# Twelve slots for split weights instead of thirteen, six raw weight buffers instead of four

## What is computed

```
h = RMSNorm(x);  proj = h @ w_in
o_gla  = gated linear attention(proj), chunks of 64, 4 heads, state carried over 16 chunks
o_diff = differential attention(proj), 4 heads, two softmax maps per head
x = x + concat(norm(o_gla) * silu(gate), norm(o_diff) * silu(gate)) @ w_out
k, v = RMSNorm(mem) @ w_ckv
x = x + softmax(RMSNorm(x) @ w_cq @ k^T) @ v @ w_co
out = RMSNorm(x)
```

## Time and profile before

| | |
|---|---|
| median of 3 runs | 870.24 us (870.15 to 870.57) |
| the profiled execution: its own time | 874.1 us |
| its span, first to last instruction | 872.4 us |
| TensorE matmul busy | 850.4 us, 97% |
| DVE busy | 529.6 us, 61% |
| ACT busy | 397.2 us, 46% |
| DMA queue of the data | 66.85 MB, 24.2% of 16 engines |
| granted TensorE clock, mean | 0.996 |

### The profile page before, as it was taken

The page is one execution under the profiler, slowest core; times in us unless marked ns, Lnnn a source line. Parts: engine busy times, 40 slices in busy tenths (PEclk is TensorE's granted clock), DMA queues, the critical chain, the costliest instruction groups (busy, mean ns, idle before and its releaser), DMA issues.

```text
span 872.4 us, 12997 instructions
## 1 busy us (share of the span) xinstructions
PE 850.4 (97%) x4676; PEld 705.0 (81%) x4676; DVE 529.6 (61%) x1274; ACT 397.2 (46%) x982; POOL 44.1 (5%) x84
## 2 busy tenths in 40 slices
PE   7999999999999999999999899999999999999997
PEld 6777877777788888888878887888888888888885
DVE  6667667767578668678768765223336654355543
ACT  7765444444346345445545655203425543234422
POOL 2000000000000000000000000000100000010001
PEclk9999999999999999999999999999999999999999
DMA  8321112112212112102112266521022202351112
GB/s 270 110 78 37 31 41 69 37 43 67 59 31 55 35 34 56 34 22 67 43 63 74 88 213 216 184 86 61 32 89 74 68 29 73 97 192 49 49 49 97
DMA packets 53592, 67.69 MB, mean 78 GB/s; under 512 B 5844, under 2 KB 32536, under 8 KB 53528
## 3 DMA queue, kind: packets, MB, share of 16 engines
q1 hardware_dynamic: 53528, 66.85, 24.2%
HBM read 58.44 MB, written 8.39 MB: 77 GB/s over the span
## 4 chain that ended last, share of the span: by engine, by line
PE 78%; DVE 11%; ACT 4%; issue 3%; DMA 3%; POOL 0%; SPq 0%; POOLq 0%; ACTq 0%
PE bank L1350 12%; PE bank L1352 12%; PE bank L1351 12%; PE banks2to L1350 8%; PE banks2to L1352 8%; PE banks2to L1351 8%; PE banks6to L1401 4%; PE banks2to L1573 4%; PE bank L1599 2%; DVE w_lo L1004 2%; DVE state L1183 1%; ACT junk L789 1%; ACT w_hi L793 1%; DMA tile_a<-mixed 1%; DVE mix_out L1207 1%
## 5 line engine op out<-in xcount | busy, mean ns | idle before, releaser
L1350 PE MATMUL bank<-w_hi,actT_hi 128*128 128x512 f32 x472 | 189.8, 402 | 1.2 <-DVE gate L1161 0.3
L1352 PE MATMUL bank<-w_hi,actT_lo 128*128 128x512 f32 x472 | 184.5, 391 | 0.0
L1351 PE MATMUL bank<-w_lo,actT_hi 128*128 128x512 f32 x472 | 184.3, 390 | 0.0
L1004 DVE SCALAR_TENSOR_TENSOR w_lo<-w_raw,vecs,w_hi 128x512 fp32r<-128x512 f32 x120 | 86.6, 747 | 43.5 <-ACT w_hi L793 43.5
L1350 PEld LDWEIGHTS bank<-w_hi,actT_hi 128*128 128x128 f32 x472 | 88.9, 188 | 22.2 <-DVE gate L1161 3.5
L1352 PEld LDWEIGHTS bank<-w_hi,actT_lo 128*128 128x128 f32 x472 | 88.6, 188 | 19.2
L1351 PEld LDWEIGHTS bank<-w_lo,actT_hi 128*128 128x128 f32 x472 | 88.9, 188 | 16.6
L793 ACT ACTIVATE w_hi<-w_raw,vecs 128x512 fp32r<-128x512 f32 x120 | 82.4, 717 | 11.8 <-DMA w_raw<-in_w_cq 6.1
L1350 PE MATMUL banks2to<-w_hi,actT_hi 128*128 128x512 f32 x168 | 66.5, 396 | 0.0
L1352 PE MATMUL banks2to<-w_hi,actT_lo 128*128 128x512 f32 x168 | 65.6, 390 | 0.0
L1351 PE MATMUL banks2to<-w_lo,actT_hi 128*128 128x512 f32 x168 | 65.5, 390 | 0.0
(11 more groups left out here) (288 smaller groups left out, 1818.9 us busy)
## 6 DMA issues: line engine op xcount, KB each, us to landing
w_raw<-in_w_in SPq DMA_DIRECT2D x56, 256.0 KB, 2.9
w_raw<-in_w_ckv SPq DMA_DIRECT2D x32, 256.0 KB, 3.4
w_raw<-in_w_cq SPq DMA_DIRECT2D x32, 256.0 KB, 2.8
w_raw<-in_w_co SPq DMA_DIRECT2D x32, 256.0 KB, 2.7
stage_in<-in_x SPq DMA_DIRECT2D x8, 512.0 KB, 4.9
tile_a<-mixed SPq DMA_DIRECT2D x16, 256.0 KB, 3.6
w_raw<-in_w_out SPq DMA_DIRECT2D x16, 256.0 KB, 3.1
x_res<-in_x SPq DMA_DIRECT2D x8, 512.0 KB, 4.9
```

Of the source, the lines that this page charges most:

```text
L1004: return dve.scalar_tensor_tensor(dst, src, scale, hi.bitcast(F32), ALU.mult, ALU.subtract)
L1350: pe.matmul(dst, l_hi, r_hi, start=start, stop=False)
L1351: pe.matmul(dst, l_hi, r_lo, start=False, stop=False)
L1352: return pe.matmul(dst, l_lo, r_hi, start=False, stop=stop)
```

## The change

Two constants change. A slot is w_hi and w_lo of a tile, 2 x 2 KB in each partition, and a raw buffer is 2 KB, so the memory that is given up and taken is the same.

```
-NW = 13
-NRAW = 4
+NW = 12
+NRAW = 6
```

## The result

The changed kernel takes 876.04 us (median of 4 runs, 875.55 to 876.53) against 870.19 us of the kernel before on the same chip (4 runs, 869.77 to 870.57): ratio 1.0065, 95% interval 1.005 to 1.0079. It is slower by 5.85 us, where 2.1 was forecast, and beyond the upper end of the range. The profiled execution of it took 875.55 us, its span is 873.8 us and its mean granted clock 0.999.

A forecast was written before the change was run, and what follows sets the result against it. The prediction took TensorE as the bound nearly everywhere. Costs of +4.15 us (+1.33 - 0.50 + 2.0 + 0.66 + 0.66) and gains of -2.05 (-1.2 - 0.85) gave +2.1 on 870.24: 872.3 us, range 869.6 to 874.7.

The forecast's parts named there:

- +1.33 - 0.50 = 0.83: GLA passes: a fourth w_lo at either end costs 1.33 us; one step per pass without a w tile returns 0.50.
- the price of a place: Bunches on TensorE's path at GLA ends, head turns, groups 6 to 7 and 14 to 15: 0.66 us per added w_lo.
- All other bunches of four: Bunches at X, C, the other Q, and V: w_lo keeps up with TensorE, so they cost 0.
- the -1.2 and the half of -1.7 against it: tile_a wait near 529 us: earlier load gives -1.2 us; avoided half clock gives -1.7, counted half as -0.85.
- rival A: Wait and clock dip near 529 us are not in timed runs, or tile lands as late: 874.4 us; chance 0.23.
- The step on the load's start: Last tile_a load starts 1.1 to 1.2 us earlier; gain bounds 0, if the tile lands as late, and -2.0.
- a wait that the prediction counted as 0: Earlier tile_a waits at 509.55 and 513 us: gain counted as 0, ends 0 and -1.1.
- The signs that the prediction named: Third tile_a wait 0.5 to 1.0 us, clock 1.00 through 531 to 535; a remaining dip would point to A.
- the clock "stayed": Clock did not fall behind waits of 1.2 us at 492.28 and 0.85 at 509.55, so 0.8 should keep it.
- Rival B: Everything in the last transfer's shadow returns, with the clock: +0.45, 870.7 us, no change; chance 0.24 together with D.
- rival C: Stage 478 to 545 us: 5.4 us idle and 1.7 dip could go, against 4.15: -2.9, 867.3 us; chance 0.08.
- Rival D: The three turns of a head absorb their tile: sum +0.1, 870.3 us; chance 0.24 together with B.

The follow-up runs named there:

- second profile of the kernel before: The kernel before, unchanged, traced a second time: 870.87 us against 870.63, ratio 1.0003, span 869.1 us.
- places alone: The kernel before with thirteen slots and four raw buffers kept, tiles placed as for twelve slots: 878.62 us, ratio 1.009 to the kernel before.
- the tile put back: The changed kernel with the second early tile of groups 4, 5 and 6 behind E 1 instead of E 2: 876.16 us, ratio 1.006 to the kernel before.
- the second set: Experiments on the cost terms one by one; its yardstick, the changed kernel unchanged, took 877.65 us, ratio 1.0074 to the kernel before.
- the load ahead of the tiles: The kernel before with tiles 80 to 82 placed behind the load of tile_a in SP's queue: 870.07 us, ratio 0.9995.
- slots alone: The kernel before with twelve slots instead of thirteen, raw buffers left at four: 877.37 us, ratio 1.0082.
- the fifth tile ahead of the last projection: The changed kernel with the fifth tile of groups 2 and 3 ahead of a GLA pass's last projection: 877.7 us, ratio 1.0077 to the kernel before.
- three places eased: The changed kernel with E 1 restored, a group 7 tile behind PV 28, tile_a's load ahead of tiles 80 to 82: 876.25 us, ratio 1.0058 to the kernel before.

## Why the prediction was wrong

The places at which the same matmul stands in the second profile of the kernel before and in the profile after give the cost stretch by stretch. Rows of the second profile of the kernel before:

```profile
212.94 0.35 PE L1524 MATMUL banks6to<-v,sc_hi 128*128 128x256 f32 x1 [0.58 <-issue]
...
409.73 0.39 PE L1351 MATMUL bank<-w_lo,actT_hi 128*128 128x512 f32 x1
...
488.59 0.39 PE L1599 MATMUL bank<-dv,prT_hi 128*128 128x256 f32 x1 [0.26 <-DVE prT_lo L1003]
```

and of the kernel after:

```profile
213.87 0.36 PE L1524 MATMUL banks6to<-v,sc_hi 128*128 128x256 f32 x1 [1.24 <-issue]
...
413.58 0.39 PE L1351 MATMUL bank<-w_lo,actT_hi 128*128 128x512 f32 x1
...
493.13 0.39 PE L1599 MATMUL bank<-dv,prT_hi 128*128 128x256 f32 x1
...
513.01 0.66 PE L1401 MATMUL banks6to<-ident,tile_a 128*128 128x128 f32 x4 [0.49 <-DMA tile_a<-mixed]
```

The next pair is 528.87 and 532.87, shown above, and the last the two spans, 869.1 and 873.8. The lag is how much later the kernel after is at the same matmul.

| stretch | lag at its end | cost of it | forecast |
|---|---|---|---|
| start and GLA | 0.93 | 0.93 | +1.33 - 0.50 = 0.83 |
| heads | 3.85 | 2.92 | 2.0 |
| groups 6 to 7 | 4.54 | 0.69 | 0.66 |
| the memory's values, to 529 us | 4.00 | -0.54 | -1.2 - 0.85 = -2.05 |
| the rest, with groups 14 to 15 | 4.70 | 0.70 | 0.66 |
| sum | | 4.7 | 2.1 |
| timed | | 5.85 | |

**Right: the price of a place.** Where a w_lo joins a bunch on TensorE's path it costs 0.66 us. It did so at either end of a GLA pass, at three turns of a head, at groups 6 to 7 and at groups 14 to 15. All seven places were named beforehand, and each measures 0.62 to 0.70 us between the two traces. At groups 14 to 15 the wait that grew is the one of 0.44 us, not the one of 0.57 that the prediction read; the price is the same. The 0.50 that the GLA steps give back came as well. That the stricter `w_used` costs nothing was right too, as the kernel with the places alone shows.

**Wrong: a term is missing, for the tiles that move singly.** The step "All other bunches of four" looked at the bunches and at nothing else. The table of the change has the second early tile of groups 4, 5 and 6 move from E 1 to E 2, and the sum has no term for it. The timelines of ACT tell what it does. In the second profile of the kernel before, and then in that after:

```profile
237.80 0.20 ACT L933 ACTIVATION_READ_ACCUMULATOR prob<-banks2to,neg_maxs 128x1 f32 x1
237.97 0.38 ACT L793 ACTIVATE qkT_hi<-banks6to 128x256 fp32r<-128x256 f32 x1
```

```profile
238.69 0.20 ACT L933 ACTIVATION_READ_ACCUMULATOR prob<-banks2to,neg_maxs 128x1 f32 x1
238.79 0.72 ACT L793 ACTIVATE w_hi<-w_raw,vecs 128x512 fp32r<-128x512 f32 x1
239.40 0.38 ACT L793 ACTIVATE qkT_hi<-banks6to 128x256 fp32r<-128x256 f32 x1
...
241.59 0.33 ACT L793 ACTIVATE qk_tok<-banks2to 128x192 f32<-128x192 f32 x1 [1.81 <-PE banks2to L1352]
```

w_hi stands behind the exponentials. DVE waits for it with w_lo, and behind that come the inverse sums, the combined map and `qkT_lo`, as the timeline of DVE in the profile after has it:

```profile
239.54 0.75 DVE L1004 SCALAR_TENSOR_TENSOR w_lo<-w_raw,vecs,w_hi 128x512 fp32r<-128x512 f32 x1 [0.83 <-ACT w_hi L793]
...
240.72 0.62 DVE L1260 SCALAR_TENSOR_TENSOR prob<-prob,map_ratio 128x384 f32<-128x384 f32 x1
241.26 0.41 DVE L1003 TENSOR_TENSOR qkT_lo<-banks6to,qkT_hi 128x256 fp32r<-128x256 f32 x1
```

In the second profile of the kernel before `qkT_lo` starts at 239.09, 2.2 us earlier, 1.3 us with the lag of 0.9 taken off; the wait is what is left of that. Three heads, about 0.35 net each: 1.04 us in the trace of the changed kernel with the tile put back, 0.9 the other way round in the kernel before. This is the 0.9 by which the heads cost more than forecast.

**Wrong: the -1.2 and the half of -1.7 against it.** They were read from a wait of 1.86 us and a fall of the clock in a trace 3.9 us longer than the median. The prediction gave this case as rival A and half a term, and gave A 0.23. The second trace shows 0.68 us and no fall. The step on the load's start was right: the load starts at 524.91 in the second profile of the kernel before and at 527.66 in the changed one, which lags 4.0 us there, so 1.3 us earlier (forecast 1.1 to 1.2). But it took 5.17 us instead of 3.91 with it, as the lower bound of that step had it. (The 3.66 us that the prediction gives as ACT's wait for tile 82 are the transfer's own time; ACT waited 1.77 us for tile 81 and 0.35 for tile 82.) At this wait, then, the change gave 0.04 us between the two traces that are compared here, and 0.64 in the second trace of the changed kernel, where TensorE doesn't wait there at all. The scatter of one transfer is as large as the term.

The -0.54 of the table comes from elsewhere, from a wait that the prediction counted as 0: ahead of the first of these loads TensorE waits 1.53 us in the second trace of the kernel before and 0.49 in that after, which is 1.05 us, and 0.56 of it is lost again at the next load, at 516.93. The two terms were -2.05, the stretch gave -0.54: 1.5 us. The signs that the prediction named could not have told: a wait of 0.57 us and a clock of 1.00 from 531 to 535 us came as forecast, but the second trace of the kernel before has much the same.

The Trainium skill (DMA: Bandwidth & Descriptors, Anatomy of one DMA) has 256 KB at 2.6 us by its formula for the GpSimd path. The loads here come from SyncE's queue: those of `tile_a` that TensorE waited for took 3.8 to 5.8 us in the four traces of the two kernels, so the formula doesn't fit them.

**Not in the forecast: what lies between traces and timed runs.** The traces account for 4.7 us, the timed runs for 5.85, and for some 6.4, by the ratio, in the second set. Of the 1.2 us between, 0.7 are that the second trace of the kernel before took 870.87 us and its median in the first comparison is 870.19; 0.5 are that the trace after took 875.55 and its median is 876.04. In the runs of the result this isn't the clock: three of the four have a mean clock of 0.999, that is at most 1.3 us lost, and a fall costs 1.7. What it is stays open; the kernel's medians also differ from set to set (870.19 to 870.94 before, 876.04 and 877.65 after).

In the later sets the clock does play a part. The prediction argued that the clock "stayed" behind waits of 1.2 and 0.85 us in one trace, and that waits of the costs add up and no more. The runs show falls of 1.7 us behind waits of 1.21 and 1.50 us, which the change makes or lengthens, in one traced execution and not in another of the same waits. Three such waits are new or longer: two of 1.2, one of 1.5. That falls make the longer ones of the timed runs there is the reading that fits the two groups of spans; it isn't shown run by run, as timed runs have no trace.

So 3.75 us of error are 1.5 for the trace's stall and clock, 0.9 for E 2, 1.2 for how the two traced executions lie to their medians, and the rest small. Rival A, 874.4, was nearest; with the term for E 2 it gives 875.3. Rival B and rival C counted on the same stall and fell with it. Rival D fell too: the turns of a head absorb nothing, and could not be made to by moving the tile.

No version here is shown to beat the kernel before; the one with the load ahead of the tiles can't be told from it. Both sides of its setting lose, and on different work: a slot less costs on DVE wherever a group turns, a raw buffer less costs transfers in the one stage that lives on them.

## What to carry to other kernels

When a constant moves places in a hand-made order, list every item that moves, the single ones too, and look for each at what stands behind it on both engines that it occupies; the step with no slack was one place further on. A term that gives time back should be held against the gap between the traced execution and the median before it goes into the sum: if the trace is longer than the runs by as much as the term, take the case without it as the likeliest, or read a second trace. And a new wait of a microsecond on TensorE can cost more than itself.

## What the runs showed of the hardware

In the traces of the kernels with four or six raw buffers, each fall of the granted clock to 1.2 GHz in mid-kernel cost 1.7 us. It fell behind waits of 1.21 us (148.53, places alone), 1.50 us (484.22, the tile back at E 1), 1.94 us (534.44, slots alone) and 1.86 us (530.49, first trace of the kernel before), and behind two waits of 0.76 and 0.34 us close together (207.04 and 207.97, the fifth tile ahead of the last projection). It didn't fall behind waits of 1.21 and 1.50 us at the same places in both traces of the changed kernel, nor behind 1.53 us (509.53, second trace of the kernel before), 1.68 us (535.95, places alone) and 1.76 us (484.86, three places eased). So the length of the wait alone doesn't decide: a wait of this size makes the loss of 1.7 us possible, not certain.

A load of `tile_a` (256 KB) behind the same instruction took 5.17, 3.91 and 5.17 us in the first and second trace of the kernel before and the first of the changed one. An earlier one took 5.83 us, the load that ends ahead of 509.53 in the second trace of the kernel before.
